# A decoder trunk step on one Trainium2 core: another order at the opening, three weight tiles split on VectorE instead of through GpSimd, and an earlier turn in the tail

## The reference

```python
x = x + 0.5 * swiglu(rms_norm(x, g_ffn1), w1_ffn1, w3_ffn1, w2_ffn1)
z = rms_norm(x, g_mix) @ w_in + b_in
# window attention with sinks on q, k, v; gated chunk mixing on u, vg
x = x + concatenate([attn_out, gm_out]) @ w_out + b_out
x = x + 0.5 * swiglu(rms_norm(x, g_ffn2), w1_ffn2, w3_ffn2, w2_ffn2)
x = x + sigmoid(rms_norm(x, g_ple) @ w_ple_gate) * (ple @ w_ple_proj)
y = rms_norm(x, g_final)

def swiglu(x, w1, w3, w2):
    return (silu(x @ w1) * (x @ w3)) @ w2
```

## Time and profile before

| what | value |
|---|---|
| median of 3 runs | 934.61 us (934.48 to 934.86) |
| the profiled execution's own time | 936.01 us |
| its span, first to last instruction | 933.1 us |
| PE busy | 921.6 us, 7659 matmuls |
| DVE, ACT, POOL busy | 749.3, 593.5, 228.6 us |
| transfers | 133 MB, mean 143 GB/s |

### The profile page before, as it was taken

The page is one execution under the profiler, slowest core; times in us unless marked ns, Lnnn a source line. Parts: engine busy times, 40 slices in busy tenths (PEclk is TensorE's granted clock), DMA queues, the critical chain, the costliest instruction groups (busy, mean ns, idle before and its releaser), DMA issues.

```text
span 933.1 us, 19735 instructions
## 1 busy us (share of the span) xinstructions
PE 921.6 (99%) x7659; PEld 911.6 (98%) x7659; DVE 749.3 (80%) x1295; ACT 593.5 (64%) x1032; POOL 228.6 (25%) x178
## 2 busy tenths in 40 slices
PE   7999999999999999999999999999999999999997
PEld 7999999999999999999999999999999999999997
DVE  6979977888888787667876488997788888879785
ACT  7758755776676674666545466866667667757443
POOL 0212222223222310000318412222222322222221
PEclk9999999999999999999999999999999999999999
DMA  8958888777977778312124696887787887777912
GB/s 251 177 104 166 158 158 171 144 133 157 186 151 140 125 163 225 75 47 68 46 77 118 123 194 141 160 169 153 151 157 132 173 164 155 144 153 173 182 48 92
DMA packets 252688, 133.07 MB, mean 143 GB/s; under 512 B 15610, under 2 KB 248724, under 8 KB 252580
## 3 DMA queue, kind: packets, MB, share of 16 engines
q1 hardware_dynamic: 178164, 93.75, 35.9%
q0 software_dynamic: 74096, 37.23, 32.4%
q10 hardware_dynamic: 336, 0.84, 0.2%
HBM read 129.24 MB, written 3.59 MB: 142 GB/s over the span
## 4 chain that ended last, share of the span: by engine, by line
PE 96%; DVE 1%; DMA 1%; SPq 0%; ACT 0%; issue 0%; DVEq 0%
PE ps L2174 61%; PE ps L2085 27%; PE ps L2203 2%; PE ps L2119 2%; PE ps L2526 1%; PE ps L2536 1%; DMA x_rows<-in_x_prompt_dram 1%; PE ps L2391 1%; PE ps L2420 1%; SPq L790 0%; PE ps L2440 0%; PE ps L2499 0%; PE ps L2507 0%; PE ps L2464 0%; PE ps L2447 0%
## 5 line engine op out<-in xcount | busy, mean ns | idle before, releaser
L2174 PE MATMUL ps<-xo_hi,w_lo 128*128 128x260 f32 x1008 | 284.7, 282 | 0.0
L2174 PE MATMUL ps<-xo_hi,w_hi 128*128 128x260 f32 x1008 | 284.4, 282 | 0.0
L2174 PE MATMUL ps<-xo_lo,w_hi 128*128 128x260 f32 x864 | 244.1, 283 | 0.0
L1548 DVE TENSOR_TENSOR w_lo<-w_raw,w_hi 128x512 fp32r<-128x512 f32 (+1 forms) x180 | 176.2, 984 | 23.3 <-ACT w_hi L971 18.7
L2174 PEld LDWEIGHTS ps<-xo_hi,w_lo 128*128 128x128 f32 x1008 | 190.1, 189 | 0.0
L2174 PEld LDWEIGHTS ps<-xo_hi,w_hi 128*128 128x128 f32 x1008 | 189.7, 188 | 0.0
L2174 PEld LDWEIGHTS ps<-xo_lo,w_hi 128*128 128x128 f32 x864 | 162.6, 188 | 0.0
L2174 PE MATMUL ps<-hop_hi,w_hi 128*128 128x260 f32 x560 | 158.5, 283 | 0.0
L2174 PE MATMUL ps<-hop_hi,w_lo 128*128 128x260 f32 x560 | 158.4, 283 | 0.0
L2174 PE MATMUL ps<-hop_lo,w_hi 128*128 128x260 f32 x560 | 158.2, 282 | 0.0
L1312 POOL DMA_DIRECT2D w_lo<-in_w_ffn_dram x60 | 76.8, 1280 | 286.1 <-ACT w_lo L982 286.1
(11 more groups left out here) (371 smaller groups left out, 2069.4 us busy)
## 6 DMA issues: line engine op xcount, KB each, us to landing
w_lo<-in_w_ffn_dram POOLq DMA_DIRECT2D x88, 256.0 KB, 5.5
w_a<-in_w_ffn_dram SPq DMA_DIRECT2D x36, 512.0 KB, 5.5
w_a<-in_w_ffn_dram SPq DMA_DIRECT2D x60, 256.0 KB, 2.9
w_raw<-in_w_ffn_dram SPq DMA_DIRECT2D x44, 256.0 KB, 4.5
w_raw<-in_w_ffn_dram SPq DMA_DIRECT2D x20, 512.0 KB, 6.0
w_a<-in_w_ffn_dram SPq DMA_DIRECT2D x48, 192.0 KB, 3.0
w_lo<-in_w_ffn_dram POOLq DMA_DIRECT2D x32, 192.0 KB, 5.3
w_raw<-in_w_in_dram SPq DMA_DIRECT2D x10, 512.0 KB, 4.7
```

The lines of the kernel that those rows point to most:

```text
L1548: nc.vector.tensor_tensor(w_cells(wl, s, j, name, n), w_cells(w_raw, s, j, name, n), w_cells(wh, s, j, name, n).bitcast(F32), ALU.subtract ...
L2174: ins = pe.matmul(ps[:, b, 0:Q], w[:, cc, k * P:(k + 1) * P], m_, start=(first and k == 0 and t == 0), stop=(k == kn - 1 and t == 2), skip ...
```

## The change

The opening takes the tokens in two parts instead of the features: row blocks 2 and 3 are loaded first, whole, then the first weight tile in two transfers of four pieces, then blocks 0 and 1, then the second weight tile. PE turns block 2, the samples and block 3, then block 0 and 1 among the products of the first tile (`first_unit`), whose two token halves are made one after the other; `second_unit` makes the high-part products ahead of the low-part ones. Some matmuls on constants are added (`keep_busy`). The squares of a block are summed over whole rows. The spreading of the norm's factor moves from the second tile to the third, behind its second piece.

In the second FFN the low parts of tiles 6 and 7, and of the first projection tile of the last block, are subtracted by DVE instead of being summed by a transfer of POOL.

In the tail `turn_middle(0)` runs before the sums of squares, and `middle_rows(0)` before `token_gated(1)`; the first output block is stored as columns 512 to 1023 and 0 to 511.

```diff
-X_BANK = (2, 3, 4, 5, 6, 4, 5, 7)
...
+FIRST_TOKENS = (slice(256, 512), slice(0, 256))
+X_BANK = ((4, 5, 6, 7), (2, 3, 4, 5))
@@ which tiles go which way
-        summed += [("up", 1, n) for n in range(3, N_STD)] + last_keys(1)[:2] + last_keys(1)[3:6]
+        summed += [("up", 1, n) for n in range(3, N_STD - 2)] + last_keys(1)[:1] + last_keys(1)[3:6]
-        next_first = last_keys(0)[1:3] + last_keys(1)[2:3]
+        next_first = last_keys(0)[1:3] + [("up", 1, n) for n in range(N_STD - 2, N_STD)] + last_keys(1)[1:3]
@@ SP, opening
-            for h, landed in enumerate((x_in, x_in_right)):
-                for b in range(NB):
-                    part = slice(h * 512, (h + 1) * 512)
-                    sp_.dma_start(x_rows[:, b, part], a["x_prompt"][0, b * P:(b + 1) * P, part]).then_inc(landed[b], 16)
-                if h == 0:
-                    load(("up", 0, 0), w_dram["w1_ffn1"][:, :, 0:P])
-            load(("up", 0, 1), w_dram["w3_ffn1"][:, :, 0:P])
+            for n, blocks in enumerate(((2, 3), (0, 1))):
+                for b in blocks:
+                    sp_.dma_start(x_rows[:, b, :], a["x_prompt"][0, b * P:(b + 1) * P, :]).then_inc(x_in[b], 16)
+                src = std_source(("up", 0, n))
+                if n:
+                    load(("up", 0, n), src)
+                else:
+                    c = cell[("up", 0, 0)]
+                    for j, landed in enumerate((first_w_in, raw_in[slot[("up", 0, 0)]])):
+                        sp_.dma_start(w_raw[:, c + j, :].rearrange("p (k c) -> p k c", k=4), src[:, 4 * j:4 * j + 4, :]
+                                      ).then_inc(landed, 16)
@@ ACT, opening
+            first_hi(0, 0)
+            first_hi(0, 1)
+            act.wait_ge(first_w_in, 16)
+            nc.scalar.activation(wh[:, c, :], w_raw[:, c, :], ACT.Copy).then_inc(first_w_hi, 1)
+            first_hi(0, 2)
+            first_hi(0, 3)
+            act.wait_ge(raw_in[slot[("up", 0, 0)]], raw[("up", 0, 0)])
+            nc.scalar.activation(wh[:, c + 1, :], w_raw[:, c + 1, :], ACT.Copy).then_inc(w_hi_ready, 1)
+            for k in range(4, KD):
+                first_hi(0, k)
+            x_copy(0, 0)
+            x_copy(0, 1)
+            for k in range(KD):
+                first_hi(1, k)
             split_hi(("up", 0, 1))
+            x_copy(1, 0)
+            x_copy(1, 1)
+            x_copy(0, 2)
+            x_copy(0, 3)
+            act.wait_ge(x_in[0], 16)
+            act.wait_ge(row_sums, 1)
+            nc.scalar.activation(sq_rows[:, 1, :], x_rows[:, 0, :], ACT.Square, accum_out=rs_t[:, 0:1]).then_inc(row_sums, 1)
             split_hi(("up", 0, 2))
+            x_copy(1, 2)
+            x_copy(1, 3)
@@ POOL: which tiles it leaves to others
-                if key in first_out or key in first_up:
+                if key in first_out or key in first_up or key in next_first:
@@ DVE: the step ("w", "up", n) now has work of its own
-                    elif kind == "lo" and std_key(s, arg) in next_first:
+                    elif kind in ("lo", "w") and std_key(s, arg) in next_first:
                         key = std_key(s, arg)
                         dve.wait_ge(w_hi_ready, index[key] + 1)
                         nc.vector.tensor_tensor(w_at(wl, key), w_at(w_raw, key), w_at(wh, key).bitcast(F32),
@@ DVE, opening
+            row_square(2)
...
+            for k in range(4):
+                first_x_lo(0, k)
             first_lo(0)
+            for k in range(4, KD):
+                first_x_lo(0, k)
+            for k in range(KD):
+                first_x_lo(1, k)
             first_lo(1)
+            row_square(1)
+            row_square(3)
+            first_lo(2)
             stat_rsqrt(0)
...
-            first_lo(2)
             first_lo(3)
-            dve.wait_ge(x_by_act, 6)
+            dve.wait_ge(x_by_act, 8)
@@ DVE, tail
             token_rows(0)
+            middle_rows(0)
             token_gated(1)
             dve.wait_ge(y_turned, 2)
-            middle_rows(0)
             token_add(1)
@@ PE, opening
+            pe.wait_ge(consts_ready, 2)
+            keep_busy(3)
...
+            keep_busy(6)
+            pe.wait_ge(x_in[2], 16)
+            for j in range(4):
+                turn_first(0, 2, j)
...
+            pe.wait_ge(x_in[3], 16)
+            for j in range(4):
+                turn_first(0, 3, j).then_inc(x_turned, 1)
+            keep_busy(3)
+            def first_unit():
+                early, late = range(4), range(4, KD)
...
+                pe.wait_ge(x_in[1], 16)
+                for j in range(2):
+                    turn_first(1, 1, j).then_inc(x_turned, 1)
+                lo_wait(pe, key)
+                first_products(0, 1, early, (2,))
+                for j in range(2, 4):
+                    pe.wait_ge(x_by_act, j - 1)
+                    turn_first(1, 0, j)
+                    turn_first(1, 1, j).then_inc(x_turned, 1)
+                first_products(0, 1, late, (2,))
+                for k in late:
+                    pe.wait_ge(first_lo_ready, k + 2)
+                    first_products(0, 1, (k,), (1,), last=k == KD - 1)
+                for k in range(KD):
+                    pe.wait_ge(xg_hi_ready, k + 1)
+                    first_products(0, 0, (k,), (0, 2), first=k == 0)
+                for k in range(KD):
+                    pe.wait_ge(xg_lo_ready, k + 1)
+                    ins = first_products(0, 0, (k,), (1,), last=k == KD - 1)
+            def second_unit(vectors):
+                pe.wait_ge(w_hi_ready, index[key] + 1)
+                pe.wait_ge(x_by_act, 4)
...
@@ PE, third tile of the first FFN
+                                pe.wait_ge(x_by_act, 8)
+                                between = [(2, first_stat_out)]
@@ PE, tail
             turn_rows(0)
+            pe.wait_ge(xf_ready, N_WHOLE)
+            turn_middle(0)
...
-            turn_back(0, Y_BANKS[0], range(N_WHOLE - 1))
-            pe.wait_ge(x_ready, 24 + KD + 1)
-            turn_middle(0).then_inc(y_turned, 1)
+            turn_back(0, Y_BANKS[0], range(N_WHOLE - 1)).then_inc(y_turned, 1)
+            pe.wait_ge(y_right_ready, 2)
             turn_rows(1).then_inc(y_turned, 1)
```

More of the change, by code:

```diff
@@ L1069, in first_hi @@
[L1069 to L1083, removed]
@@ L1084, in _, with first_hi @@
-            split_hi(("up", 0, 1))
[L1085 to L1090, removed]
+            act.wait_ge(cols_ready, 1)
+            def first_hi(part, k):
+                act.wait_ge(x_turned, 4 * part + k // 2 + 1)
+                nc.scalar.activation(h_hi[:, k, FIRST_TOKENS[part]], x_turn(part, k), ACT.Copy, scale=col(k)
+                                     ).then_inc((first_hi_ready, xg_hi_ready)[part], 1)
@@ new lines, in x_copy @@
+            def x_copy(part, j):
+                act.wait_ge((first_lo_ready, xg_lo_ready)[part], 2 * j + 3 - part)
+                nc.scalar.activation(x[:, 2 * j:2 * j + 2, FIRST_TOKENS[part]], x_bank(part, j), ACT.Copy
+                                     ).then_inc(x_by_act, 1)
+            c = cell[("up", 0, 0)]
+            first_hi(0, 0)
+            first_hi(0, 1)
+            act.wait_ge(first_w_in, 16)
+            nc.scalar.activation(wh[:, c, :], w_raw[:, c, :], ACT.Copy).then_inc(first_w_hi, 1)
@@ L1266, in _ @@
             y_rows(1)
[L1267 to L1268 removed]
+            act.wait_ge(y_right_ready, 4)
+            act.wait_ge(y_ready[1], 1)
             act.dma_start(o["y_prompt"][0, P:2 * P, :], y[:, 1, :]).then_inc(out_done, 16)
@@ L2218, in ffn_stage @@
                         n, = arg
+                        if s == 0 and n < 2:
+                            if n:
+                                second_unit(vectors)
+                            else:
+                                first_unit()
+                            continue
                         ready, between = None, []
@@ L2256, in ffn_stage, with keep_busy, turn_first @@
                         ins.then_inc(p_turned, 1)
+            def keep_busy(n):
+                for _ in range(n):
+                    pe.matmul(ps[:, 0, 0:P], ones[:], ones[:], start=True, stop=True)
+            def turn_first(part, b, j):
+                for k in range(2 * j, 2 * j + 2):
+                    ins = turn(x_turn(part, k)[:, b % 2 * P:(b % 2 + 1) * P], x_rows[:, b, k * P:(k + 1) * P])
+                return ins
+            pe.wait_ge(consts_ready, 2)
+            keep_busy(3)
@@ new lines, in _, with first_products @@
+            for j in range(4):
+                turn_first(0, 3, j).then_inc(x_turned, 1)
+            keep_busy(3)
+            def first_products(n, h, ks, parts, first=False, last=False):
+                for k in ks:
+                    c, w0 = cell[("up", 0, n)] + k // 4, k % 4 * P
+                    for i in parts:
+                        w, m_ = ((wh, h_hi), (wh, h_lo), (wl, h_hi))[i]
+                        ins = pe.matmul(ps[:, 2 * n + h, 0:HALF], w[:, c, w0:w0 + P], m_[:, k, h * HALF:(h + 1) * HALF],
```

(17 more changed lines are left out.)

130 lines of the change are left out of this document (49 added, 81 removed).

## The result

After: 942.25 us, median of 4 runs (941.51 to 943.71), against 934.55 (934.13 to 934.86) before on the same chip: ratio 1.0079, 95% interval 1.0067 to 1.0091, so 7.2 us slower (6.3 to 8.5). Forecast: 938.8, with a range to 940.9. Measured again with the later experiments the ratio was 1.0067 (1.0054 to 1.0079), 6.2 us slower. Both lie above the forecast's 4.2. The profiled execution took 941.77, its span is 940.0 (before: 933.1).

A forecast was written before the change was run, and what follows sets the result against it. PE was taken as the bound, busy 921.6 of 933.1 us. Opening -0.6, second FFN +4.9 and tail -0.15 made +4.2 us, on the median 934.61 + 4.2 = 938.8, with a range of 936.4 to 940.9.

The forecast's parts named there:

- The opening: Start of the first FFN: second tile at 18.7, third at 24.6; 0.6 us gained, bounds 1.1 gained to 0.1 lost.
- I take 12.89 for it again: Opening: x's last block lands at 12.89 us as before, since 2.5 MB still have to land ahead of it.
- The place: Second FFN: DVE stands from 537.37 to 545.9 ahead of tile 6's subtraction, holding PE 4.9 us in all.
- ACT gets the raw tile only at 544.80: Second FFN: tile 6's load lands then, ACT's rounding ends at 545.86, and DVE's subtraction has to wait for it.
- after this PE is as late as DVE but for 1.1, which is the distance of before: Second FFN, behind `comb` 0: PE already held 4.9 us, so no third stall follows the stalls of 2.1 and 2.8.
- 6.1 if PE inherits the whole lag: Second FFN: upper bound of PE's loss, in us, beside the forecast 4.9 and the lower bound 2.1.
- The projection tile: Last block: DVE's added subtraction ends p's low part at 868.3, before PE leaves the first gate tile at 869.5; costs nothing.
- The tail: End of kernel: `middle_rows` 0 leaves the last chain, 0.27 gained; one turn moves ahead, 0.12 lost; net 0.15 us gained.
- absorbed: Rival, second FFN: DVE's wait costs PE nothing, opening and tail gains remain; -0.75, 933.9 us; chance 0.07.
- first stall only: Rival, second FFN: DVE catches up before `comb` 0, so PE loses 2.1 less 0.75; 936.0 us; chance 0.08.
- the opening loses: Rival, opening: ACT's chain, later landing, tile 4's transfer or low clock takes back 0.6 and 1 us more; 940.4; chance 0.13.
- Larger transfers land sooner: Rival, opening: whole row blocks of x land sooner, ACT's 18.2 decides, 1.1 us gained; 938.3 in all; chance 0.12.

The follow-up runs named there:

- kernel 1: Kernel after with the low parts of up tiles 6 and 7 and projection tile 0 given back to negation and accumulating transfer; 1.0001 over the kernel before.
- experiment 4: Kernel after with DVE's subtractions of tiles 6 and 7 moved ahead of `swi_b` 1 in the second FFN; 1.0002 over the kernel before.
- experiment 5: Kernel before with DVE waiting for tile 6's rounding ahead of the second FFN's `swi_b` 0, subtracting nothing; 1.0038 over the kernel before.
- experiment 9: Kernel after with PE's code 128 instructions longer, by waits on a count long reached in the first FFN's products; 1.0044 over the kernel before.
- experiment 2: Kernel before with only the three low parts moved to DVE; 1.0058 over the kernel before.
- experiment 6: Kernel after with 12 constant matmuls on PE in its wait ahead of the second FFN's first product; 1.0063 over the kernel before.
- experiment 10: Kernel after with the three low parts given back to negation and transfer, plus 128 reached waits on PE; 0.9991 and 0.9992 over the kernel before.
- experiment 11: Kernel before with 48, 24, 36, 6 or 12 reached waits added to PE's code; 0.9999, 1.0000, 0.9998, 0.9996, 0.9992 over the kernel before.

## Why the forecast came out too low

**The opening** (-0.6). The numbers are right: second tile 18.62 (18.7 forecast), third 24.57 (24.6), start -0.48. DVE's roots ended at 25.25 (25.3), POOL issued tile 4's transfer at 25.71 (25.9), and PE lost nothing up to 37 us. The way to them is not: "I take 12.89 for it again", of the landing of x's last block, was wrong. SP issued that load at 3.30, with five loads ahead of it, not at 5.67 with eight, and it landed at 10.89:

```profile
x_rows<-in_x_prompt_dram SPq DMA_DIRECT2D x1, 512.0 KB, 7.6
```

PE turned that block only at 12.95, because it stood behind ACT's roundings, and these behind PE's own first turns. PE's turns of the first block, in the kernel after and in kernel 1:

```profile
5.71 1.83 PE L2121 MATMUL ps<-ident,x_rows 128*128 128x128 f32 x8
```

```profile
5.16 1.04 PE L2121 MATMUL ps<-ident,x_rows 128*128 128x128 f32 x8
```

They start 0.21 apart in the first and 0.11 in the second. The trace records the granted clock as 1.00 from 7.3 us on in the first and from 4.6 on in the second. So an earlier landing and slower turns cancelled, and that the sum came out is luck. It also scatters: the start lies at 59.43 to 60.55 in the nine profiles with the old opening (mean 60.08), each time 47.5 to 47.6 behind x's last landing, and at 58.63 to 60.19 in the nine with the new one (59.66), where the two lowest are those whose first turns ran 0.11 apart. The difference of the means is -0.42.

**The place.** Right: DVE stood where I said, for the reason I gave, and experiments 4 and 5 show that it is this. Its length was 9.57, not 8.5: I took the load's 5.30 of before as fixed, and it took 6.44. This is the first failed step, "ACT gets the raw tile only at 544.80": 1.1 of the 2.0 missing. Experiment 9 takes it away with nothing changed in the opening or the lists; that it is the packet that does it rests on the two groups of profiles there.

**The reserve.** The second failed step is "after this PE is as late as DVE but for 1.1, which is the distance of before". I gave DVE 1.92 + 0.26 + 2.59 of idle time and PE this 1.1, 5.87 together; the line says 5.03. The missing 0.84 is this 1.1, which is the margin at one check, `comb` 0, and a later check has less. PE can start product 7 of the fourth unit only when ACT's second `snap` of that unit is done. ACT's `snap` and PE's first matmul of that product before, then in the kernel after:

```profile
604.75 0.37 ACT L1006 ACTIVATE snap<-ps 128x260 f32<-128x260 f32 x1
```

```profile
605.55 0.28 PE L2174 MATMUL ps<-xo_hi,w_hi 128*128 128x260 f32 x1
```

```profile
611.36 0.38 ACT L1017 ACTIVATE snap<-ps 128x260 f32<-128x260 f32 x1
```

```profile
611.88 0.36 PE L2176 MATMUL ps<-xo_hi,w_hi 128*128 128x260 f32 x1
```

Before, PE comes 0.43 behind the end of `snap`. After, it comes 0.14 behind, as it does wherever it waits for one, and so in all seven profiles of the table with a loss. So 0.28 was spare, and 1.92 + 0.26 + 2.59 + 0.28 = 5.05 is the line's 5.03. With the load on time (experiment 9) PE's delay against before is 2.3 behind `w_lo`, 3.9 behind the first unit's `snap`, 5.06 behind `comb` 0, 5.3 behind the second unit's `snap` and 5.57 behind the fourth's, and stays there. So the forecast's 4.9 was right to 0.2 as far as `comb` 0, and "no third stall" missed two small ones. My bound "6.1 if PE inherits the whole lag" was the likelier value; with the late load it is 7.1, and 6.90 was measured.

**The form.** I said two waits, 2.1 and 2.8. After had one of 3.2 and a stretch at half clock; in experiments 2, 6 and 9 the clock stayed up and the later waits appeared (2.0, 1.4 and 0.9 in experiment 9). The size is the same by the same line.

**The projection tile** (0): right; DVE ends the low part of p at 874.69, and PE's first gate tile runs from 870.10 for 5.8 us.

**The tail** (-0.15): right, -0.16. But "how they are cut costs nothing; the last store still hangs on DVE's last instruction" was incomplete: the last store also hangs on what its 16 engines still have to move, and that took 0.7 more in the first profile of after, 0.2 more in the second. Why is shown only in part (experiments 10 and 11).

**Sum** as measured: -0.48 + 6.90 - 0.16 + 0.70 = 6.96, less the 0.06 outside the columns 6.9 of span, against 6.2 to 7.2 in the two sets of runs. The rivals: "absorbed" and "first stall only" are out (the earlier trace rows were the right argument against the second), "the opening loses" too as I meant it. "Larger transfers land sooner" is out by its time, 938.3, but its condition came true: x was in 2.0 us sooner. Whether the size of the transfers did that or only their earlier issue isn't tested. Its bound, ACT's fourth copy, ended at 18.48 (18.2 forecast), and the second tile began at 18.62, where PE's own pace would have had it at 18.58: both came out together. In kernel 1, with the faster first turns, it began at 17.30.

## What to carry to other kernels

When a wait is put into an in-order list, add up its idle spots up to the next thing that the bound engine asks for, add the smallest margin that the bound engine has at any later check, on every engine that is fed from that list (here 0.28 at ACT's `snap`, not 1.1 at the next check), and count the whole rest of the lag as lost. Moving the instruction behind the work that doesn't need it (experiment 4) made the same three subtractions free. A term that comes out right in the sum is not thereby right: look whether the wait that it names was there (the opening). And a change of the instructions of one engine can shift when its later code is loaded: before a difference under 1 us is given to an edit, measure the kernel with its code lengthened by reached waits.

## What the hardware showed that I had not expected

- PE's granted clock fell to 0.50 in the wait of 3.2 us, for 6.8 us, in both profiles of the kernel after; after waits of 2.4 and 2.0 us (middle alone, after with longer code) it stayed at 1.00. It cost nothing by itself, since PE would have waited for DVE and ACT instead (experiment 6). The Trainium skill (TensorE: Matmul & The Clock Gate, section Part 1: The HAM clock gate) has these two levels, 1.2 GHz when TensorE has been idle and 2.4 when it has been busy; the trace agrees with 0.22 and 0.12 us for the same matmul.
- The code packet of 16 KB in experiment 10 takes 1.27 us of one DMA engine, and behind it the last store trailed at the pace of one or two engines. The Trainium skill (DMA: Bandwidth & Descriptors, section iDMA fabric) says, in a remark on loads that it marks as an unconfirmed explanation, that a bulk load runs at the pace of its slowest engine; the six slices of experiment 10 agree for a store: 15 to 44 GB/s, where all 16 engines together move some 410, or 26 each. The packets' place goes with 1.0 us in an accumulating transfer and 1.1 in the load behind it (experiment 9 moves both), and with 1.5 in the last store (experiment 10).
- Five kernels that differ from the kernel before only by reached waits (6 to 48 on PE) lie within 0.1% of it.
- x's last block landed at 10.8 to 11.2 us in the nine profiles with four loads of 512 KB, and at 11.9 to 13.0 in the nine with eight of 256 KB; the order of the loads differs too.
